# First norm's weight as one row, copied to all partitions in PSUM by two float32 products, in a one-core hybrid attention and convolution layer

## What is computed

```python
h_res = jnp.concatenate([meta, x], axis=1)      # 528 rows of 1024
hn = rms_norm(h_res, norm_mix_gain[l])          # row * rsqrt(mean(row^2) + eps) * gain
part = lambda i: hn @ w_l[:, o[i]:o[i + 1]]     # q, k, v, forget gate, GLU, two gates
u = glu_in[..., :D_CONV] * jax.nn.sigmoid(glu_in[..., D_CONV:])
```

## Time and profile before

| | |
|---|---|
| median of three runs | 921.69 us (920.42 to 923.43) |
| profiled execution, its own time | 920.88 us |
| its span, first to last instruction | 918.9 us |
| PE busy | 907.6 us, 99% |
| DVE busy | 620.4 us, 68% |
| ACT busy | 450.9 us, 49% |
| mean granted TensorE clock | 0.997 |

### The profile page before, as it was taken

The page is one execution under the profiler, slowest core; times in us unless marked ns, Lnnn a source line. Parts: engine busy times, 40 slices in busy tenths (PEclk is TensorE's granted clock), DMA queues, the critical chain, the costliest instruction groups (busy, mean ns, idle before and its releaser), DMA issues.

```text
span 918.9 us, 13783 instructions
## 1 busy us (share of the span) xinstructions
PE 907.6 (99%) x5079; PEld 791.9 (86%) x5079; DVE 620.4 (68%) x963; ACT 450.9 (49%) x725; POOL 22.3 (2%) x40
## 2 busy tenths in 40 slices
PE   7999999999999999999999999999999999999997
PEld 7999999999999999888888888888888888888886
DVE  7699989999999999986766656543444344434543
ACT  6432236787778777666843444422342134215523
POOL 2010000000000000010000000000000000000000
PEclk9999999999999999999999999999999999999999
DMA  9333332222222222212335333333233333333502
GB/s 258 98 93 95 84 88 82 61 57 69 69 59 56 69 69 58 80 55 84 114 90 185 92 92 92 92 101 105 86 100 94 105 87 103 92 101 105 161 1 92
DMA packets 154043, 84.36 MB, mean 92 GB/s; under 512 B 3103, under 2 KB 151583, under 8 KB 154000
## 3 DMA queue, kind: packets, MB, share of 16 engines
q1 hardware_dynamic: 152768, 82.32, 31.3%
q10 hardware_dynamic: 640, 1.18, 0.4%
q0 software_dynamic: 592, 0.29, 0.2%
HBM read 81.62 MB, written 2.16 MB: 91 GB/s over the span
## 4 chain that ended last, share of the span: by engine, by line
PE 95%; DVE 2%; ACT 1%; DMA 1%; issue 1%; ACTq 0%; DVEq 0%
PE pj L1367 61%; PE pj L1363 18%; PE pQ L1507 3%; PE pQ L1490 3%; PE pj L1669 2%; PE pQ L1669 2%; PE pj L1405 1%; PE pQ L1477 1%; PE pQ L1476 1%; DVE cv L1002 1%; PE pQ L1510 1%; DMA u<-in_norm_mix_gain_dram 1%; PE pQ L1384 1%; PE pj L1416 0%; PE pj L1518 0%
## 5 line engine op out<-in xcount | busy, mean ns | idle before, releaser
L551 ACT ACTIVATE w_hi<-raw 128x1024 fp32r<-128x1024 f32 x129 | 135.8, 1052 | 137.2 <-PE pj L1367 108.2
L1367 PE MATMUL pj<-in_hi,w_lo 128*128 128x512 f32 x512 | 201.8, 394 | 0.0
L1367 PE MATMUL pj<-in_hi,w_hi 128*128 128x512 f32 x512 | 201.1, 393 | 0.0
L1367 PE MATMUL pj<-in_lo,w_hi 128*128 128x512 f32 x512 | 201.1, 393 | 0.0
L907 DVE TENSOR_TENSOR w_lo<-raw,w_hi 128x1024 fp32r<-128x1024 f32 x129 | 157.6, 1222 | 35.4 <-ACT w_hi L551 35.1
L1002 DVE SCALAR_TENSOR_TENSOR cv<-u,prm,cv 128x512 f32<-128x512 f32 x240 | 170.8, 747 | 0.5
L1367 PE MATMUL pj<-mid_hi,w_hi 128*128 128x512 f32 x320 | 125.7, 393 | 0.0
L1367 PE MATMUL pj<-mid_hi,w_lo 128*128 128x512 f32 x320 | 124.6, 389 | 0.0
L1367 PE MATMUL pj<-mid_lo,w_hi 128*128 128x512 f32 x320 | 124.5, 389 | 0.0
L1367 PEld LDWEIGHTS pj<-in_hi,w_hi 128*128 128x128 f32 x512 | 96.3, 188 | 20.4 <-issue 0.6
L1367 PEld LDWEIGHTS pj<-in_lo,w_hi 128*128 128x128 f32 x512 | 96.2, 188 | 18.4 <-issue 0.5
(11 more groups left out here) (202 smaller groups left out, 1144.9 us busy)
## 6 DMA issues: line engine op xcount, KB each, us to landing
raw<-in_w_in_dram SPq DMA_DIRECT2D x57, 512.0 KB, 3.8
raw<-in_w_mlp_up_dram SPq DMA_DIRECT2D x32, 512.0 KB, 4.0
raw<-in_w_mlp_down_dram SPq DMA_DIRECT2D x32, 512.0 KB, 3.7
raw<-in_w_attn_out_dram SPq DMA_DIRECT2D x8, 512.0 KB, 3.7
raw<-in_w_conv_out_dram SPq DMA_DIRECT2D x8, 512.0 KB, 3.6
raw<-in_w_out_dram SPq DMA_DIRECT2D x8, 512.0 KB, 3.7
ga<-in_x_dram SPq DMA_DIRECT2D x4, 512.0 KB, 8.5
cv<-in_x_dram SPq DMA_DIRECT2D x1, 2048.0 KB, 9.5
```

What stands on the lines that cost most here:

```text
L551: A(w_hi[:, c % SPLIT, :], raw[:, c % RAW, :], ACT.Copy).then_inc(s_hi, 1)
L1367: last = mm(prod(c), wt, src[:, at:at + NT], **flags)
```

## The change

The weight vector is loaded once, as one row of 4 KB on partition 0, first in ACT's queue, ahead of the meta tokens. The two broadcast loads go. PE multiplies a row of ones (1 x 128) by that row in two float32 products of 512 columns each, so that all 128 partitions of two PSUM banks (`gain_all`, the second half of `pj`) hold the weight; `scale_tokens` reads it there and waits for the new semaphore `s_gp`. Because those banks are now taken, the meta tokens' transposes and the parameters' transposes move to the first half of `pj`, the last token group is transposed ahead of `half_tile(1, 0)` and not inside it, and two waits are added on PE. The `keep_busy` transposes are dealt out anew (4, 8, 4, 6 for 20 and 5). ACT makes the first weight chunk's high part ahead of the tokens' high parts, DVE its low part one place earlier, and the parameters' copy out of PSUM moves ahead of the last tokens' high part.

```diff
-        gain_in = u[:, D:2 * D]
-        gain_meta = u[0:META, 2 * D:3 * D]
+        gain_row = u[0:1, D:2 * D]
+        gain_all = pj[:, 1, :]
...
             if t == QT:
-                return pj[:, 1, 0:KT * META].rearrange("p (m t) -> p m t", t=META)
+                return pj[:, 0, 0:KT * META].rearrange("p (m t) -> p m t", t=META)
...
-        pPrm = pj[:, 1, 512:512 + KT * NR]
+        pPrm = pj[:, 0, 512:512 + KT * NR]
...
-                if t == 0:
-                    sp.dma_start(gain_in, norm_mix_gain[0].partition_broadcast(P)).then_inc(s_g1, 16)
...
+            act.dma_start(gain_row, norm_mix_gain).then_inc(s_g1, 16)
             act.dma_start(x_meta, meta_tokens[:, :]).then_inc(s_x[QT], 16)
-            act.dma_start(gain_meta, norm_mix_gain[0].partition_broadcast(META)).then_inc(s_gm, 16)
...
+            high(0)
             in_high(0, ORDER[0])
             in_high(1, ORDER[1])
-            high(0)
             in_high(2, ORDER[2])
...
             in_high(3, ORDER[3])
-            in_high(4, ORDER[4])
             act.wait_ge(s_pT, 1)
             A(prm[:, :], pPrm, ACT.Copy).then_inc(s_sig, 1)
+            in_high(4, ORDER[4])
...
-                dve.wait_ge(s_g1 if t < QT else s_gm, 16)
+                dve.wait_ge(s_gp, 1)
...
-                                       in1=gain_in if t < QT else gain_meta, op0=ALU.mult, op1=ALU.mult).then_inc(s_xs, 1)
+                                       in1=gain_all[0:n, :], op0=ALU.mult, op1=ALU.mult).then_inc(s_xs, 1)
...
             in_low(0, ORDER[0])
+            low(0)
             in_low(1, ORDER[1])
-            low(0)
...
-            keep_busy(20)
+            keep_busy(4)
+            pe.wait_ge(s_one, 1)
+            pe.wait_ge(s_g1, 16)
+            for half in range(2):
+                last = mm(gain_all[:, half * NT:(half + 1) * NT], f_one[0:1, 0:P],
+                          gain_row[:, half * NT:(half + 1) * NT], start=True, stop=True)
+            last.then_inc(s_gp, 1)
+            keep_busy(8)
             tokens_transpose(0, ORDER[0])
+            keep_busy(4)
             tokens_transpose(1, ORDER[1])
-            keep_busy(5)
+            keep_busy(6)
             tokens_transpose(2, ORDER[2])
...
+            pe.wait_ge(s_inlo, 1)
             half_tile(0, 0, (0, 2, 1))
             tokens_transpose(3, ORDER[3])
-            half_tile(1, 0, (0, 2, 1), lambda: tokens_transpose(4, ORDER[4]))
+            tokens_transpose(4, ORDER[4])
+            half_tile(1, 0, (0, 2, 1))
+            pe.wait_ge(s_sig, 1)
             half_tile(0, 1).then_inc(s_mm, 1)
-            pe.wait_ge(s_sig, 1)
             half_tile(1, 1).then_inc(s_mm, 1)
```

More of the change, by code:

```diff
@@ L335, in build @@
         s_g1 = sem("s_g1")
-        s_gm = sem("s_gm")
+        s_gp = sem("s_gp")
         s_again = sem("s_again")
@@ L1389, in keep_busy @@
                 for _ in range(n):
-                    nc.tensor.transpose(pj[:, 0, 0:P], ident[:, :], ident[:, :])
+                    nc.tensor.transpose(pj[:, 0, D - P:D], ident[:, :], ident[:, :])
             def half_tile(c, h, order=(0, 1, 2), between=None):
```

## The result

The change made the kernel slower by a little: 922.89 us (922.09 to 923.54, 14 runs) against 921.3 us (920.12 to 923.43, 14 runs), ratio 1.0016, 95% interval 1.0009 to 1.0024. The forecast was 1.0 us faster. Repeated later on another chip the changed kernel gave 922.93 us, ratio 1.0021 (1.0012 to 1.0030). The difference is under the 0.3% that I had called the bound of no change, but it has the other sign and is clear of the measurement's interval. The profiled execution spans 920.1 us against 918.9; the prediction had 917.9, so the whole error of 2.2 us lies in the span.

What follows compares the result with a forecast made beforehand. Bound: prologue plus PE's own work. Group 4 2.1 us earlier, less a 0.97 us pass and 0.1 for hand-overs, saves 1.0: 920.88 becomes 919.9 profiled, 920.7 with the median's 0.8; range 919.7 to 921.7, with rivals 919.2 to 922.9.

Steps and rivals of the forecast that it cites:

- The step that failed: PE's prologue: two one-row products end at 6.55 us with the clock rising at 6.1; group 2 transposed 10.8 to 11.7.
- Rival 1: PE's clock at half through groups 1 and 2: first product at 14.75, end 0.5 us later, 922.2 us; chance 0.18.
- The start of the scaling: DVE's meta tokens' scaling: row lands at 3.4 us, products end at 6.55, scaling starts at 6.6 against 6.66.
- The broadcast loads: SP's queue: without the broadcast, group 2's x and the first weight chunk land 1.7 us earlier, the chunk at 9.65.
- Rival 3: First weight chunk lands only 0.47 us earlier, at 10.9; the gain is gone, 922.0 us; chance 0.10.
- Reading the weight in PSUM: DVE's scalings: an operand in PSUM costs nothing visible, 1.23 us against 1.22 with both in SBUF.
- Group 4 ahead and `high(0)` first: New order: group 4 starts 2.1 us earlier with a 0.97 us pass still behind it; `high(0)` runs 9.65 to 10.7.
- Rival 2: Weight's row lands late: break-even with products ending at 7.7 us; at a 5.8 us landing time, 923.9 us; chance 0.12.
- Rival 4: Clock falls again and the first `half_tile` runs at half: 2.1 us later, 923.8 us; chance 0.05.
- The rule of the Trainium skill: PE's clock: transposes don't count as activity, so filling is vain; the prediction said the earlier trace disagrees, level 0.97 at 12.80.

Runs made afterwards that it cites:

- e3_rows_1: Kernel before with its 20 first keep_busy transposes replaced by 12 float32 products of one row by 512 columns; span 933.3 us, one execution.
- e12_products_128: Changed kernel with its two float32 products made of 128 rows, the weight replaced by a pattern; 920.36 us, ratio 0.9997 to the kernel before.
- e2_no_fill: Changed kernel without the 18 keep_busy transposes behind the two products; 922.07 us, ratio 1.0007 to the kernel before.
- e10_no_products: Changed kernel without the two float32 products, weight left out, row still loaded and waited for; 922.93 us, ratio 1.0015 to the kernel before.
- e8_row_on_sp: Changed kernel without the 18 fillers, the row's load moved to the front of SP's queue; 922.0 us, ratio 1.0007 to the kernel before.
- e7_no_weight: Kernel before without both broadcast loads, the norm's weight left out; 919.99 us, ratio 0.9988.
- e5_group4_first: Kernel before with only group 4 transposed ahead of half_tile(1, 0); 921.37 us, ratio 0.9998.
- e6_high_first: Kernel before with only the first weight chunk's high part moved ahead and its low part one place earlier; 921.08 us, ratio 0.9995.
- e1_meta_first: Changed kernel with the meta tokens' load issued ahead of the weight's row; 924.65 us, ratio 1.0030 to the kernel before.
- e13_more_fill: e11_transposes_and_fill plus two keep_busy in PE's wait for the copy of the weight's columns; 920.2 us, ratio 0.9992 to the kernel before.
- e11_transposes_and_fill: e9_broadcast_by_transposes plus seven keep_busy behind the weight's transposes and one between groups 0 and 1; 920.44 us, ratio 0.9992 to the kernel before.
- e9_broadcast_by_transposes: e8_row_on_sp with the products replaced by transposes of the weight's columns, each read 128 times over; 921.5 us, ratio 0.9999 to the kernel before.
- e4_rows_128: As e3_rows_1, but with all 128 rows in each of the 12 products; span 923.8 us, one execution.
- e16_more_fill_again: The kernel of e13_more_fill timed once more; 919.66 us, ratio 0.9980 to the kernel before.

## Why the prediction was wrong

**The step that failed** is the one on the new products: "if it rises at 6.1 as it did before", and after it "Group 2 is transposed from 10.8 to 11.7 at full clock". I carried the moment at which the level rose from a profile in which PE ran 128-row transposes over to one in which it runs one-row products. In e3_rows_1 20.8 us of these didn't raise it, and the level that they left behind made the first twelve fillers and group 1 take nearly twice as long as in e12_products_128. A second term was missing with it: the sum has no time for the eighteen fillers behind the products, as if PE always had idle time for them, and on the chain they took 3.7 us. Group 2 was turned at 13.36 instead of 10.8, the first product came at 15.60 instead of 13.2, and group 4 at 19.78 instead of 17.5: that last 2.3 us is the error of the span. Of the 2.4 us at the first product, 128 rows in the products gave back 1.9 (13.72 in e12_products_128); 0.5 are left for the later start of the scaling. Without the eighteen fillers and with one-row products it came at 14.68 (e2_no_fill). The time of e12_products_128 was 920.36, ratio 0.9997.

**Rival 1** had this outcome and too small a price. It gave 0.5 us for half level through groups 1 and 2; the spans gave 1.2 and the medians 1.6. It kept the scaling's start at 6.6, and in it the eight and four fillers ahead of group 1 cost nothing; on the chain they are 1.90 and 1.04 us. I had argued against the rival that PE "now has products and `keep_busy` in just that stretch". The stretch was indeed filled: PE had no pause from 2.36 us to group 1, and the level was half all the same. One of its signs, a granted clock of 0.50 in 9 to 13 us, did not show, since the windows view says 1.00 for that whole stretch (more on this below); the other, a first product behind 14 us, did.

**The start of the scaling** was forecast at 6.6 and came at 7.31. The products began at 3.41 (forecast 3.4), right behind the four transposes, so the row was there by then; how much earlier the trace doesn't show, so no run decides between 2.65 us for it and the 2.0 us and bytes of the Trainium skill (DMA: Bandwidth & Descriptors, the anatomy of one DMA), which that section fits to transfers that POOL issues, where this one is ACT's. They ended at 7.19 where the sum had 6.5 with a rise and 6.85 without: the last instruction's own length, 1.06 us and not a step of 0.86, had been left out, and that is 0.2 of the 0.34 us. And a second cause was not in the sum at all: the meta tokens' load, moved to second place, landed at 5.5. Every DMA of a moved step was to be counted, and I counted the load that came ahead, not the one that it pushed back. It ended level with the products, so that it cost nothing by itself, but hid any gain from shorter ones (e10_no_products); an early load alone gave nothing either (e8_row_on_sp).

**The broadcast loads.** The mechanism was right and its size too small: the chunk came at 1.66 + 7.0 = 8.7 us (forecast 9.65), 2.6 us earlier than before, not 1.7. Rival 3, 0.47 us only, is refuted with it, and the removal alone is 1.1 us (e7_no_weight). **Reading the weight in PSUM** costs nothing: 1.28 us a scaling of 128 rows, against 1.28 and 1.29 before. **Group 4 ahead and `high(0)` first** cost nothing alone (e5_group4_first, e6_high_first). **Rival 2**, the row itself late, did not happen in the changed kernel. Its break-even, products ending at 7.7 us, was too late: they ended at 7.19, and the kernel was 1.6 us slower all the same. In e1_meta_first they ended at 8.9, and it was 3 us above the kernel before. **Rival 4**, the half level in the first `half_tile`, was not in the changed kernel's profiles; it was in those of e6_high_first and e8_row_on_sp, where the first pass took 2.10 us.

**The rule of the Trainium skill** (TensorE: Matmul & The Clock Gate, PE-mode transpose), that transposes don't count as activity for the clock, disagrees with these runs as it did with the earlier trace rows. In e13_more_fill PE ran nothing but transposes up to 7 us, and seven fillers took 0.93 us, which is the full level:

```profile
5.98 0.93 PE L1394 MATMUL pj<-ident 128*128 128x128 f32 x7
```

Not in every execution: in e11_transposes_and_fill the same seven took 1.70 us at 6.05, and the level stayed half through groups 1 and 2 as well. So transposes can bring the level up, and the runs don't say when. The prediction weighed that question for transposes and did not ask it of the one-row products, which stayed at half throughout.

## What to carry to other kernels

A broadcast by a one-row product looks cheap and wasn't early in this kernel: it ran at half the clock, the clock was still at half behind it, and whatever was queued behind it paid again. Transposes of a column read many times over made the same copy in 1.97 us against 3.78; with the weight's own transpose, DVE's copy and the wait for it, they ended 2.84 us behind the start, 0.9 us sooner (e9_broadcast_by_transposes). Put fillers only where PE is idle in the profile, and take their price at the half level. When something is put ahead in a queue, follow what it pushes back. And one profile is not the kernel: the same lines moved by 0.9 us between two profiles of the changed kernel (first product at 15.60 and 16.50).

## What the runs showed of the hardware

- **One-row products did not bring the clock up (e3_rows_1, e4_rows_128, e12_products_128).** 24 float32 instructions of one row by 512 columns, back to back over 20.8 us, all took 1052 ns or more; with 128 rows they fell to 592 ns near 6 us. With 128 rows in the changed kernel's own products, all that came behind them from 6.69 us on ran at the full level.
- **The granted clock of the windows view can't be trusted from the start of a kernel.** For the one-row products it says 1.00 over the whole stretch (columns: window, length, busy and count of PE, PEld, DVE, ACT and POOL, granted clock, DMA share, GB/s), while each instruction took the time of the half level. In the changed kernel it says 1.00 while group 1's transposes take the 1.92 us of the half level. It seems to show a level only from its first recorded change on. The durations of equal instructions tell it:

```profile
2.36:23.00 20.64, 20.64 (x24) 7.92 (x25) 5.90 (x7) 5.02 (x11) 4.08 (x8) 1.00 0.82 237
```

- **The moment at which the level rises can differ between executions**: 12.8 us in the kernel before, about 17.5 in e6_high_first, and between two profiles of the changed kernel six fillers from 12.59 us took 0.94 and 1.49 us. The profiles of e13_more_fill and e16_more_fill_again, again one kernel, agree. One profile is one sample of it.
- **A small load came late when it was not in front.** The same 4 KB row was there by 3.4 us when issued at 0.76, and at 5.1 when issued at 1.21, behind the meta tokens (e1_meta_first, one profile).
